# Routing gates of a mixture layer: a gate matrix built by one-hot products, or by GpSimd adding single gates into cleared DRAM

## The reference

```
q = (x @ w_q).reshape(bsz, t, 8, 2, 128)                 # 8 heads, 2 halves
s = einsum('bthcd,cnd->bthcn', q, sub_keys)              # 128 keys a half
top_s, top_i = top_k(s, 16)                              # 16 of 128, each half
cand_s = top_s[..., 0, :, None] + top_s[..., 1, None, :] # 256 candidates
best_s, best_pos = top_k(cand_s, 16)                     # 16 experts of 16384
gate = softmax(best_s)
act = gelu(x . expert_u[idx]) * gate;  ffn = sum(act * expert_v[idx])
ple = sigmoid(x @ ple_w_gate) * (p @ ple_w_proj)
x = layer_norm(ALPHA * x + ffn + ple)
```

## Time and profile before

| | us |
|---|---|
| median of 3 runs (lowest, highest) | 4457.61 (4453.36, 4460.69) |
| the profiled execution | 4456.89 |
| its span in the trace | 4455.2 |

### The profile page before, as it was taken

The page is one execution under the profiler, slowest core; times in us unless marked ns, Lnnn a source line. Parts: engine busy times, 40 slices in busy tenths (PEclk is TensorE's granted clock), DMA queues, the critical chain, the costliest instruction groups (busy, mean ns, idle before and its releaser), DMA issues. The chain is left out here.

```text
span 4455.2 us, 62361 instructions
## 1 busy us (share of the span) xinstructions
PE 4149.2 (93%) x23580; PEld 3708.6 (83%) x23580; DVE 3218.5 (72%) x4931; ACT 1562.2 (35%) x2723; POOL 702.4 (16%) x582
## 2 busy tenths in 40 slices
PE   8999989988988998899977999999999999999995
PEld 6888875656776876687767999999999999999994
DVE  4444436767846345699095889888999999888997
ACT  2112213436633321322373333333333333333332
POOL 0000001113310100334500111111111111111110
PEclk9999999989999999899999999999999999999997
DMA  9999985886686388563468999999999999999995
GB/s 276 316 313 318 309 261 164 243 236 192 204 234 207 126 273 251 176 210 134 138 177 269 311 324 321 310 313 316 313 315 320 318 316 321 314 309 320 318 315 197
DMA packets 607787, 1180.09 MB, mean 265 GB/s; under 512 B 113800, under 2 KB 360432, under 8 KB 552480
## 3 DMA queue, kind: packets, MB, share of 16 engines
q1 hardware_dynamic: 533696, 803.43, 61.1%
q0 software_dynamic: 54256, 363.92, 21.5%
q10 hardware_dynamic: 19568, 9.18, 0.8%
HBM read 1006.90 MB, written 228.15 MB: 277 GB/s over the span
## 5 line engine op out<-in xcount | busy, mean ns | idle before, releaser
L102 PE MATMUL h_ps<-h_a,h_v 128*128 128x352 f32 x6144 | 1080.6, 324 | 23.9 <-DVE h_a L96 14.0
L102 PE MATMUL h_ps<-xs,h_ut 128*128 128x352 f32 x6144 | 1079.1, 325 | 18.9 <-DVE h_ut L96 18.9
L102 PEld LDWEIGHTS h_ps<-h_a,h_v 128*128 128x128 f32 x6144 | 1005.3, 189 | 32.8 <-DVE h_a L96 19.2
L102 PEld LDWEIGHTS h_ps<-xs,h_ut 128*128 128x128 f32 x6144 | 1011.5, 189 | 19.7 <-DVE h_ut L96 19.7
L102 PE MATMUL a_ps<-xt_hi,a_w 128*128 128x512 f32 x1792 | 553.4, 390 | 7.8 <-DVE a_w L96 7.8
L96 DVE TENSOR_TENSOR h_v<-h_v_raw,h_v 128x512 fp32r<-128x512 f32 x512 | 351.5, 686 | 77.0 <-ACT h_v L95 75.7
L102 PEld LDWEIGHTS a_ps<-xt_hi,a_w 128*128 128x128 f32 x1792 | 337.3, 188 | 78.3 <-issue 8.1
L95 ACT ACTIVATE h_v<-h_v_raw 128x512 fp32r<-128x512 f32 x512 | 319.1, 624 | 222.1 <-PE h_ps L102 218.0
L102 PE MATMUL a_ps<-xt_lo,a_w 128*128 128x512 f32 x896 | 349.3, 390 | 0.0
L2794 DVE SCALAR_TENSOR_TENSOR y_first<-h_rows,h_acts,y_first 128x2048 f32<-128x2048 f32 x128 | 300.4, 2347 | 0.0
L2788 DVE CUSTOM_DVE_ANT_0 h_rows<-h_rows,h_x_first 128x2048 f32<-128x2048 f32 x128 | 292.8, 2288 | 0.0
(11 more groups left out here) (381 smaller groups left out, 6431.3 us busy)
## 6 DMA issues: line engine op xcount, KB each, us to landing
h_v_raw<-in_peer_v SPq DMA_DIRECT2D x128, 1024.0 KB
h_u_raw<-turned_d SPq DMA_DIRECT2D x144, 512.0 KB
a_raw<-in_w_in SPq DMA_DIRECT2D x28, 2048.0 KB
a_xin<-in_peer_u SPq DMA_DIRECT2D x224, 256.0 KB, 8.2
turned_d<-a_xin SPq DMA_DIRECT2D x56, 1024.0 KB, 7.3
raw_d<-in_peer_u SPq DMA_DIRECT2D x448, 128.0 KB, 3.7
h_u_raw<-raw_d SPq DMA_DIRECT2D x112, 512.0 KB
yt_last<-sums_d SPq DMA_DIRECT2D x124, 176.0 KB, 5.1
```

What stands on the lines that cost most here:

```text
L102: mm = pe.matmul(out, lhs[a], rhs[b], start=(first and n == 0), stop=(last and n == 2))
```

## The change

It does these things:

- **No gate_matrix.** A flat DRAM array `gate_flat` of 16384 x 352 values is set to zero by 11 DMAs of 2 MB from a small SBUF tile `zero`, 5 in the attention stage and 6 in finish_and_mix, on SP's queue. In route, DVE makes from each head's numbers an offset per dense token and choice (`spot`), and each head's gates at once (`lessen`, `exps`, `weigh`). GpSimd then issues, per head, 3 x 16 indirect DMAs; each adds 128 single float32 gates to `gate_flat`. Before a head's DMAs of a token block it waits for those of the head before. The stage ends when all have landed. The experts read the array as they read `sums_d`; the early-step exception with `grid_last` goes, and gathers start at slot 7 instead of 22.
- **route's order.** Queries 0 to 3 first, then two query units and two gate or projection pieces in turn, then the last pieces. POOL makes the low halves of units 2 to 6 only; DVE makes those of 0, 1 and 7 to 35, each at a fixed point between its routing instructions (`lower_due`, every fifth of 168 points from the 23rd). The sums of `base` move from POOL to DVE.
- **Layout.** `x2` is kept as `few` (160 tokens) and `xs` (352) and written so by out_project, with transposes of 32 columns each; the weights' rows are read in the same new order. A query product is therefore two matmuls, of 160 and 352 columns, where there was one of 512.
- **out_project** turns 13 blocks of `expert_u` instead of 16, all before the last piece; sums and moments of the last group go row block by row block. 3 more blocks are left to be turned by DVE in experts.
- **Low-rank halves.** `a1`'s product goes to output partitions 64 to 127, and `w2`, `a2` share one tile, `a2` on rows 64 to 127.
- **finish** takes the sum while adding (one instruction over 2048 columns), the squares on ACT, and has no statistics instructions.

```diff
-                pe.matmul(ps[0:64, 1, :], a1[:, m, :], x3[:, m % 2, 1, :], start=st, stop=en)
+                pe.matmul(ps[64:128, 1, :], a1[:, m, :], x3[:, m % 2, 1, :], start=st, stop=en)
...
-                pe.matmul(ps[:, 1, :], a2[:, c], ha[:, :], start=True, stop=True).then_inc(s["pe"], 1)
+                pe.matmul(ps[:, 1, :], wa2[64:128, c], hwa[64:128, :], start=True, stop=True).then_inc(s["pe"], 1)
...
+ZEROED, ZEROED_EARLY, ZERO_RUN = 11, 5, 256
+def clear_gates(eng, gate_flat, zero, i):
+    per = NKEY * NKEY * DENSE // P // ZEROED
+    part = gate_flat[0:NKEY * NKEY * DENSE].rearrange("(p f) o -> p (f o)", p=P)[:, i * per:(i + 1) * per]
+    return eng.dma_start(part.rearrange("p (r c) -> p r c", c=ZERO_RUN),
+                         zero[:, :].unsqueeze(1).broadcast_to([P, per // ZERO_RUN, ZERO_RUN]))
...
+            for u in ON_POOL:
+                lower(pool, u)
...
+            for h in range(PH):
+                pool.wait_ge(hd.sem, hd.at(h, "spot"))
+                pool.wait_ge(sm.sem, sm.at(h, "gate"))
+                for n in range(1, NB):
+                    if h >= 1:
+                        pool.wait_ge(put[n - 1], 16 * TOPK * h)
+                    for c in range(TOPK):
+                        pool.indirect_dma_start(
+                            gate_flat, bass.IndirectOffsetOnAxis(ap=spot[:, h, n - 1, c:c + 1], axis=0),
+                            gates[:, n, h * TOPK + c:h * TOPK + c + 1], None, compute_op=ALU.add).then_inc(put[n - 1], 16)
+            for n in range(1, NB):
+                pool.wait_ge(put[n - 1], 16 * TOPK * PH)
...
-def gate_matrix(nc, found, gates, gate_d, grid_last, last_stored, xs_d, xs):
...
+                dve.tensor_tensor_reduce(base[n][:, :], base[n][:, :], more, 1.0, 0.0, ALU.add, ALU.add,
+                                         total[:, n:n + 1]).then_inc(summed, 1)
```

More of the change, by code:

```diff
@@ L96, in split, with product @@
     return dve.tensor_tensor(lo, whole, hi.bitcast(F32), ALU.subtract).then_inc(done, 1)
-def product(pe, out, lhs, rhs, first, last):
+def product(pe, out, lhs, rhs, first, last, **how):
     for n, (a, b) in enumerate(((0, 0), (0, 1), (1, 0))):
-        mm = pe.matmul(out, lhs[a], rhs[b], start=(first and n == 0), stop=(last and n == 2))
+        mm = pe.matmul(out, lhs[a], rhs[b], start=(first and n == 0), stop=(last and n == 2), **how)
     return mm
@@ L1982, in route @@
     NR = CG * PIECE
+    pairs = [("query", 0), ("query", 1)]
+    for i in range(2, NJ // 2):
+        pairs += [("query", i), ("gate", i - 2)]
+    pairs += [("gate", i) for i in range(NJ // 2 - 2, NR // 2)]
+    units = [(kind, 2 * i + b) for kind, i in pairs for b in range(2)]
+    UNITS = len(units)
+    ON_POOL = range(2, 7)
+    LO_POINT, LO_EVERY = 23, 5
+    EXP_AT = {5: 0, 9: 1, 13: 2, 18: 3, 22: 4, 26: 5, 30: 6}
+    BASE_AFTER = {3: 0, 5: 1}
+    STORE_AT = {12: 0, 16: 1}
     with ExitStack() as ctx:
@@ L2017, in route @@
         five = "max%d index%d rest%d again%d index_again%d "
-        hd = Steps(sem("head"), 1,
+        hd = Steps(sem("head"), 2,
                    five % ((0,) * 5) + five % ((1,) * 5) + "names cand " + five % ((2,) * 5) +
-                   "shift mask float match0 match1 pick0 pick1 sum0 sum1 index index_few")
-        sm = Steps(hd.sem, hd.end(PH), "first less sum inverse gate gate_first gate_few")
-        few_idx, few_gates, few_moved = sb("few_idx", [FEW, SEL], U32), sb("few_gates", [FEW, SEL]), sem("few_moved")
@@ L2023, in route @@
-        exped, xs_stored, u_moved = sem("exped"), sem("xs_stored"), sem("u_moved")
+                   "shift mask float match0 match1 pick0 pick1 sum0 sum1 index index_few expert strided spot")
+        sm = Steps(sem("soft"), 0, "first less sum inverse gate")
+        few_idx, few_gates, few_moved = keys[0:FEW, 0, :].bitcast(U32), keys[0:FEW, 1, :], sem("few_moved")
+        second, second_kept = sb("second", [P, 2, KT, P], F32R), sem("second_kept")
+        fetched = sem("fetched")
+        exped, u_moved = sem("exped"), sem("u_moved")
@@ new lines, in w_of, with wait_raw @@
+        def w_of(h, u):
+            kind, i = units[u]
+            if kind == "query":
+                return w[h][u % 2][:, :, :]
+            return w[h][u % 2][:, :, :].rearrange("p k c -> p (k c)").rearrange("p (k c) -> p k c", c=CW)[:, 0:depth(i), :]
+        def wait_raw(eng, u):
+            b, half_of = u // 2 % 2, u % 2 if units[u][0] == "gate" else 0
+            loads = sum(1 for p in range(b, u // 2 + 1, 2) if half_of == 0 or pairs[p][0] == "gate")
+            if u == 0:
+                eng.wait_ge(query_in, 64)
+            else:
+                eng.wait_ge(raw_in[b][half_of], 64 * loads)
@@ L2285, in top16, with lower_due @@
+            points = itertools.count(1)
+            def lower_due():
+                u, late = divmod(next(points) - LO_POINT, LO_EVERY)
+                if late == 0 and u >= 0 and u + ON_POOL.stop < UNITS:
+                    lower(dve, u + ON_POOL.stop)
             def top16(c, which, keys_of, rest_of, out, out_i):
@@ L2935, in _ @@
+            invert(0)
+            for n in range(NB):
+                if n + 2 < NB:
+                    add(n + 2)
                 if n + 1 < NB:
[L2936 removed]
+                    invert(n + 1)
+                scale(n)
 def build(nc, a, out):
```

906 lines of the change are left out of this document (433 added, 473 removed).

## The result

| | before | changed |
|---|---|---|
| median, us (lowest, highest; 4 runs each) | 4459.15 (4453.36, 4463.46) | 4757.56 (4753.78, 4763.16) |
| the profiled execution | 4456.89 | 4757.25 |
| its span | 4455.2 | 4755.5 |

The changed kernel is slower: ratio 1.0671, 95% interval 1.0653 to 1.069, some 300 us. My prediction was 4455 us with a range up to 4600; the measured time lies outside it.

A forecast was written before the change was run, and what follows sets the result against it. PE bounds the experts' stage, so gains lie between stages, where GpSimd's chain would end route. 4456.9 + 20 (experts' later start) - 3 (experts) - 10 (finish) - 12 (low-rank halves) + 3 (clearing) = 4454.9, so 4455 us; range 4350 to 4600.

The forecast's parts named there:

- The step, 1.25 us: In route: each of GpSimd's 384 indirect DMAs takes 1.25 us, as the last gather distance, so the chain takes 480 us.
- rival C: In route: additions are slow, DMA engines bound from 156 ns a value; at 200 ns the total is 4589; chance 0.16.
- Rival D: In route: DVE holds GpSimd's DMAs 0.4 us each in the mean, chain 150 us longer, total 4605; chance 0.11.
- A: Main case: the step of GpSimd's chain in route between 1.12 and 1.38 us, total 4405 to 4505; chance 0.43.
- Start of the chain, 1892: In route: head 0's offsets and gates are ready and GpSimd's chain of indirect DMAs starts at 1892 us.
- PE's end in route 2225, DVE 324 us: In route: PE ends at 2225; DVE's 324 us of work fit between about 1830 and 2225; GpSimd's chain ends later.
- From the last DMA to the first matmul, 13.8 us: Between route and experts: landing adds 3.7 us, then 10.1 us from the last result to the first expert matmul.
- Experts -3: Experts' stage: `grid_last` store gone but gathers begin sooner, taken as -3 us, between -10 and +3.
- Low-rank halves -12: In rwkv_prepare: products on two halves of the PE array run side by side, -12 us, between -15 and 0.
- out_project -11: End of out_project: earlier turning and row-block sums, -11 us, between -13 and -5, already counted in the chain's start.
- finish -10: In finish: statistics and some small instructions go, 2.5 us for each of four row blocks, -10 us, between -12 and 0.
- Clearing +3: Zeroing 23 MB, with 11 more issues on SP's queue in front of weights: +3 us, between 0 and +10.

## Why the prediction was wrong

The mechanism was right: "PE and DVE now stand idle behind GpSimd". What failed is one term above all, the price of the step, which the sum multiplies by 384: "I take 1.25 us, the last distance of the same kind of instruction, so 384 x 1.25 = 480 us". The chain took 746. Of the 303 us between 4455 and 4758 the step makes 266, the start of the chain 9, the experts 9, the clearing 15, and finish with the low-rank halves 4.

- **The step, 1.25 us: wrong.** Measured 1.94: the addition 0.58, and in route another 0.22 in the mean for DVE; 384 x 0.58 + 36.4 = 259 of the 266 us by which the chain is longer; the rest is the plain step, 1.26 instead of 1.25, and rounding. I took the gather's row because it was the nearest and gave the operation no price of its own for the one thing in which it differs. The upper end was open in my text, but the case "the step between 1.12 and 1.38" stood for all prices of GpSimd's work; for the addition I thought only of the DMA engines (rival C).
- **Rival C, additions slow in the DMA engines: wrong mechanism.** Its 4589 and D's 4605 were the nearest times on record, but not for the reason that C gave. No DMA waited for the head before. Where the changed kernel runs alone, queue q0 has 23466 packets in 300 us for 163 DMAs:

```profile
q0 software_dynamic: 23466, 0.09, 23.7%
```

  That is 144 packets a DMA, and 0.237 x 16 x 300 / 23466 = 48 ns each, far from the 156 ns of C. The run with plain writes has 3808 packets for 119 DMAs, 32 each. The additions do make more transfers, but it is GpSimd's time that counts. That time does not go by the packets either: with 64 values it is 14000 packets for 176 DMAs, 80 each, and still 1.41 us. What GpSimd does in the added 0.58 us no run shows; that it builds more for an addition stays a theory.
- **Rival D, held by DVE: right in kind, a quarter in size.** 36 us and not 150. It came on top of the rest instead of being a case by itself. The worst mistake in the chances is this: A, C and D add up, and I treated them as alternatives, so the range ended at 4600.
- **Start of the chain, 1892: 1908.5.** The 1892 was counted in the times of the kernel before, without what earlier stages gain or lose; these ended 7.2 us later than there (-11.0 + 18.2, the clearing in it). In the same times route's first query came at 1805.6 instead of 1803.6 and the chain at 1901.3, 9 us late, most of it because each of the first six queries took 13.9 us and not 12.8: its 160-column matmuls cost 0.10 us and the 352-column ones 0.173, as PE's timeline in the changed kernel shows, 0.30 us for three and 0.52 for three:

```profile
1826.47 0.46 PE L102 MATMUL f_ps<-few,f_w 128*128 128x160 f32 x3
1826.77 0.68 PE L102 MATMUL f_ps<-xs,f_w 128*128 128x352 f32 x3
1827.29 0.46 PE L102 MATMUL f_ps<-few,f_w 128*128 128x160 f32 x3
```

- **PE's end in route 2225, DVE 324 us:** 2240.8, or 2233.6 in the times of the kernel before, and 313 from 1830 to 2246; neither bounds. **From the last DMA to the first matmul, 13.8 us:** 13.9.
- **Experts -3:** +6. The loads for the gathers moved in front of `expert_u` on SP's queue; I had read this part of the diff as work that became simpler, and named the gathers but not the issues on the queue.
- **Low-rank halves -12, out_project -11, finish -10:** by the borders -11.0, -12.0 (with 3 expected from route's first product, 14 together) and -7.5. By medians the parts added one after another gave 9.7, 9.6 and 5.9 us. **Clearing +3:** +17, beyond my bound of +10. The DMA shares of its stages, by windows 0.63 and 0.52, I had put at 0.7 and 0.4.

## What to carry to other kernels

In these runs an indirect DMA of GpSimd has a price that is nearly fixed whatever it moves (4 bytes or 8 KB an index, 64 or 128 values), so a scheme of single values needs the product of count and step first: here 1.16 us a step would have been the break-even with the gate matrix's end at 2352, and even plain writes miss it. Where an operation is not in the trace, price what makes it different from its nearest row by itself, and ask which engine pays. Causes that lengthen the same step add up; they are one case with a wide price, not rivals. And beside a chain of GpSimd's DMAs, look at the length of DVE's two-operand instructions.

## What was not expected of the hardware

- Adding in DRAM costs GpSimd 0.58 us a DMA more than writing, 1.54 against 0.96 us, and halving the values saves 0.13.
- A DMA of GpSimd that starts inside a wide two-operand DVE instruction is held until it ends, up to 1.98 us here (3.52 instead of 1.54); in the changed kernel none that started 0.11 us or more before it was. Four instructions of 0.69 us in place of one of 2.29 took away four fifths of what such DMAs lost (41.6 to 7.7 us), and made the chain 36 us shorter. DVE's searches and reductions (MAX8, FIND_INDEX8, MATCH_REPLACE8, TENSOR_REDUCE) held none of 33.
- The gap of 0.30 us behind each indirect DMA is the same for all four forms.
